# The opening of a two-block network: x in two column halves, and the bias vector moved behind the first weight unit

## What is computed

```
proj = x @ w_in                                   # 1024 x 2560
q_a, k_a, v_a, x_m, z_m = split(proj)
bias = rel_bias[rel_bucket(distance)]             # 32 buckets x 8 heads
logits = q_a . k_a * hd**-0.5 + bias
x_c = silu(causal_conv(x_m, conv_w, conv_b))
q_m, k_m = x_c per head @ w_qk_m;  v_m = x_m per head @ w_v_m
gates = concat(q_m, k_m, v_m) @ w_if + b_if
...
```

## Time and profile before

| What | Value |
|---|---|
| median of three runs | 2257.81 us (2256.44 to 2258.74) |
| profiled execution, its own time | 2260.36 us |
| span of its trace | 2257.3 us |
| mean granted clock of TensorE | 0.994 |
| VectorE, ScalarE and GpSimd busy | 77%, 59%, 12% of the span |
| bytes moved by DMA | 569.57 MB, mean 252 GB/s |

### The profile page before, as it was taken

How to read it: one execution, slowest core, us unless ns; L and a number is a source line. 1 busy time by engine, 2 the same in 40 slices (tenths; PEclk the granted TensorE clock), 3 DMA queues, 4 the chain that set the end, 5 groups by cost and what they waited for, 6 DMA issues and landing times.

```text
span 2257.3 us, 35008 instructions
## 1 busy us (share of the span) xinstructions
PE 2214.1 (98%) x13553; PEld 1946.6 (86%) x13553; DVE 1728.3 (77%) x1730; ACT 1333.3 (59%) x1226; POOL 265.5 (12%) x207
## 2 busy tenths in 40 slices
PE   8999999999999999999999999999999999999998
PEld 8999999999887888888888888787898999888997
DVE  5557544655788888888888888889788877798776
ACT  5643444464377777777777777676546444545444
POOL 2000000100000000000000000115193000590000
PEclk9999999999999999999999999999999999999999
DMA  9444655734599999999999999999633555434551
GB/s 295 143 141 160 205 186 185 235 127 147 174 330 360 377 368 364 377 362 378 366 376 364 374 365 377 350 362 375 221 127 113 197 175 187 152 115 160 183 195 47
DMA packets 309655, 569.57 MB, mean 252 GB/s; under 512 B 10322, under 2 KB 146244, under 8 KB 309488
## 3 DMA queue, kind: packets, MB, share of 16 engines
q1 hardware_dynamic: 303792, 548.53, 69.4%
q0 software_dynamic: 5776, 19.85, 2.7%
HBM read 562.56 MB, written 10.50 MB: 254 GB/s over the span
## 4 chain that ended last, share of the span: by engine, by line
PE 84%; POOL 5%; DVE 3%; ACT 3%; POOLq 2%; issue 1%; DMA 1%; DVEq 1%; ACTq 0%
PE ps L696 26%; PE ps L698 26%; PE ps L697 26%; POOL agT L678 3%; POOLq L677 2%; POOL tap L672 2%; DVE w_lo L1873 2%; ACT w_hi L1440 1%; PE ps L1137 1%; PE ps L763 1%; PE ps L747 1%; PE ps L910 0%; DMA xr<-rows,token_of 0%; PE ps L902 0%; PE ps L1120 0%
## 5 line engine op out<-in xcount | busy, mean ns | idle before, releaser
L1873 DVE TENSOR_TENSOR w_lo<-raw,w_hi 128x2048 fp32r<-128x2048 f32 x518 | 1194.9, 2313 | 311.7 <-ACT w_hi L1440 307.8
L1440 ACT ACTIVATE w_hi<-raw 128x2048 fp32r<-128x2048 f32 x518 | 985.8, 1908 | 330.8 <-PE ps L698 322.3
L696 PE MATMUL ps<-xT_hi,w_hi 128*128 128x256 f32 (+1 forms) x1712 | 488.6, 285 | 7.9 <-DVE xT_lo L1904 5.1
L697 PE MATMUL ps<-xT_lo,w_hi 128*128 128x256 f32 (+1 forms) x1712 | 484.0, 283 | 0.0
L698 PE MATMUL ps<-xT_hi,w_lo 128*128 128x256 f32 (+1 forms) x1712 | 484.0, 283 | 0.0
L696 PE MATMUL ps<-w_hi,xg_hi 128*128 128x512 f32 x896 | 360.5, 402 | 4.4 <-DVE w_lo L1873 4.4
L698 PE MATMUL ps<-w_hi,xg_lo 128*128 128x512 f32 x896 | 354.7, 396 | 0.0
L697 PE MATMUL ps<-w_lo,xg_hi 128*128 128x512 f32 x896 | 354.4, 396 | 0.0
L696 PEld LDWEIGHTS ps<-xT_hi,w_hi 128*128 128x128 f32 (+1 forms) x1712 | 326.3, 191 | 13.8 <-issue 7.4
L697 PEld LDWEIGHTS ps<-xT_lo,w_hi 128*128 128x128 f32 (+1 forms) x1712 | 326.4, 191 | 1.5
L698 PEld LDWEIGHTS ps<-xT_hi,w_lo 128*128 128x128 f32 (+1 forms) x1712 | 326.4, 191 | 0.4
(11 more groups left out here) (488 smaller groups left out, 2666.1 us busy)
## 6 DMA issues: line engine op xcount, KB each, us to landing
raw<-in_exp_w SPq DMA_DIRECT2D x336, 1024.0 KB, 6.1
raw<-in_ffn_w_up SPq DMA_DIRECT2D x44, 1024.0 KB, 5.1
raw<-in_w_in SPq DMA_DIRECT2D x41, 1024.0 KB, 5.9
raw<-in_ffn_w SPq DMA_DIRECT2D x33, 1024.0 KB, 5.1
raw<-in_ffn_w_down SPq DMA_DIRECT2D x22, 1024.0 KB, 5.4
raw<-in_w_gate SPq DMA_DIRECT2D x16, 1024.0 KB, 8.4
raw<-in_w_out SPq DMA_DIRECT2D x8, 1024.0 KB, 5.0
raw<-in_w_o SPq DMA_DIRECT2D x6, 1024.0 KB, 5.3
```

The source lines that it names most:

```text
L696: pe.matmul(out, lhs[0], rhs[0], start=first, stop=False)
L697: pe.matmul(out, lhs[0], rhs[1], start=False, stop=False)
L1440: act.activation(w_hi[:, u.const % SPL, 0:width], raw[:, u.const % RAW, 0:width], ACT.Copy)\
L1873: dve.tensor_tensor(w_lo[:, u.const % SPL, 0:width], raw[:, u.const % RAW, 0:width], w_hi[:, u.const % SPL, 0:width].bitcast(F32), ALU.sub ...
```

## The change

The two small tables leave the head of the sync queue and go behind the second weight half. x is loaded in two column halves of 512 KB, each ahead of one weight half, with a semaphore of its own for the second. `transpose_x` waits for the first half ahead of the first pair and for the second ahead of the third. The matmul for the bias vector moves from ahead of x to between `T(0)` and `T(1)`, into another PSUM bank (2 instead of 0), and TensorE no longer waits for its copy. ScalarE's copy moves behind the eviction of `T(0)`. GpSimd's program is untouched.

```diff
             sp.dma_start(cst[:], A["const0"]).then_inc(S_.ident_loaded, 16)
-            sp.dma_start(onehot_sb[:], A["onehot"]).then_inc(S_.table_loaded, 16)
-            sp.dma_start(relrow[:], A["rel_bias"]).then_inc(S_.table_loaded, 16)
-            sp.dma_start(x[:], A["x"][0].rearrange("(t p) d -> p t d", p=P)).then_inc(S_.x_loaded, 16)
+            x_half = lambda h: A["x"][0].rearrange("(t p) d -> p t d", p=P)[:, :, h * HALF:(h + 1) * HALF]
+            sp.dma_start(x[:, :, 0:HALF], x_half(0)).then_inc(S_.x_loaded, 16)
...
                               .then_inc(raw_landed[0] if half else S_.half_landed, 16)
+                            if half == 0:
+                                sp.dma_start(x[:, :, HALF:], x_half(1)).then_inc(S_.x_rest_loaded, 16)
+                        sp.dma_start(onehot_sb[:], A["onehot"]).then_inc(S_.table_loaded, 16)
+                        sp.dma_start(relrow[:], A["rel_bias"]).then_inc(S_.table_loaded, 16)
                         continue
...
                     if b % 2 == 0:
                         pe.wait_ge(S_.xn_ready, ready + (b // 2 + 1))
+                    if plain and b % 2 == 0:
+                        pe.wait_ge(S_.x_rest_loaded if b else S_.x_loaded, 16)
...
                 T(0, L * 12)
+                if L == 0:
+                    pe.wait_ge(S_.table_loaded, 32)
+                    pe.matmul(ps[0:HA, 2, 0:BUCKET_W], relrow[:], onehot_sb[:], start=True, stop=True).then_inc(S_.bvec_psum, 1)
                 T(1)
...
-            pe.wait_ge(S_.table_loaded, 32)
-            pe.matmul(ps[0:HA, 0, 0:BUCKET_W], relrow[:], onehot_sb[:], start=True, stop=True).then_inc(S_.bvec_psum, 1)
-            pe.wait_ge(S_.bvec_ready, 1)
-            pe.wait_ge(S_.x_loaded, 16)
...
                     out(n, xmT[:, 2 * n:2 * n + 2, CONV_K - 1:], bank(n, 2, S))
+                    if (L, n) == (0, 0):
+                        act.wait_ge(S_.bvec_psum, 1)
+                        act.activation(bvec[:], ps[0:HA, 2, 0:BUCKET_W], ACT.Copy).then_inc(S_.bvec_ready, 1)
...
-            act.wait_ge(S_.bvec_psum, 1)
-            act.activation(bvec[:], ps[0:HA, 0, 0:BUCKET_W], ACT.Copy).then_inc(S_.bvec_ready, 1)
```

## The result

| | median | ratio to before, 95% interval |
|---|---|---|
| before | 2257.81 us (7 runs) | |
| changed | 2268.63 us (7 runs) | 1.0045 [1.0034, 1.0055] |
| changed, run again (`after_again`) | 2269.70 us, before 2258.91 beside it | 1.0039 [1.0025, 1.0053] |

The change makes the kernel 10.8 us slower, in both measurements. The predicted time was 2266.4 us, in a range of 2259 to 2270. The trace read here is that of the repeat, since in the first traced execution of the changed kernel (2690.08 us, left out of the ratio) TensorE's mean granted clock was 0.752.

What follows compares the result with a forecast made beforehand. TensorE, busy 98% of the span, was taken as the bound, so the opening decides: `values` at 39.7 instead of 31.05, +8.6 us with the opening's 1.65 gain included, on the median 2257.8 gives 2266.4 us, range 2259 to 2270.

Steps and rivals of the forecast that it cites:

- part 1: Opening: x in halves lands and is transposed earlier, so T(0) ends at 17.4 instead of 19.07, a gain of 1.65 us.
- Part 2: Behind T(0): the bias vector's matmuls take 0.7 us on TensorE's path, costed at nothing because the wait for rows1 covers them.
- Part 3: GpSimd's queue before T(2): its chain starts 13.4 us later, TensorE idles about 7 us, `values` starts 8.6 us late.
- the two counts: Start of `values`: rows1 plus slow clock allow 38.8, the last b_if 39.7; the later decides, instead of 31.05.
- the second count: Before `values`: wqk, w_if and b_if are all there only when the last b_if lands, at 39.7 us.
- The rival of fast landings: GpSimd's small transfers at 19 to 31 us land in 2.0 us: 2257.7 us, no change; chance 0.15.
- The rival of useless halves: Opening: x's halves land together or late, no gain, everything 1.65 us later: +10.3 us, 2268.1; chance 0.11.
- The fixed 2.0 us: Opening loads: a fixed cost per transfer from the skill page, making x's second half an estimated 2 us late if paid in sequence.

Runs made afterwards that it cites:

- loads_ahead: Changed kernel, but GpSimd issues the ten loads (rows1, wqk, w_if, b_if) before waiting for the bias vector: 2258.24 us, ratio 0.9995 to the kernel before.
- vector_moved_alone: Kernel before with only the bias vector's matmul and copy moved behind T(0), x whole, tables at the head: 2270.85 us, ratio 1.0043.
- rows1_ahead: Changed kernel, but only the four loads of rows1 go ahead of GpSimd's wait for the vector: 2266.81 us, ratio 1.0031 to the kernel before.
- rows1_behind: Changed kernel, but wqk, w_if and b_if go ahead of GpSimd's wait and only rows1 stays behind: 2269.23 us, ratio 1.0050 to the kernel before.
- kept_busy: Changed kernel with 58 more matmuls, results unused, between T(1) and TensorE's wait for rows1: 2267.24 us, ratio 1.0040 to the kernel before.
- halves_alone: Kernel before with x in halves; tables stay at the queue's head, the vector's matmul ahead of x in PSUM bank 2, its copy not awaited: 2257.60 us, 0.9999.
- vector_between_busy: Changed kernel with ten loads ahead of GpSimd's wait, vector's matmul between x's transposes, tables before x's second half, ten extra identity matmuls: 2257.47 us, 0.9990.
- vector_between_few: Changed kernel with ten loads ahead of GpSimd's wait, vector's matmul between x's transposes, tables before x's second half, four extra identity matmuls: 2257.78 us, 0.9993.

## Why the prediction was right

**The mechanism** was the forecast one: GpSimd's queue waits for the late vector, and TensorE waits for what stands behind that wait. `loads_ahead` shows that the loss is gone when the loads stand ahead of that wait, `vector_moved_alone` that it is there without the halves. **The size** was 2.2 us short (8.6 forecast, 10.8 measured), so that the measured time lies near the top of the range: the gain of part 1 was taken too large, the time until rows1 landed and the slow clock too small, and the count that the forecast took for the later one was the earlier one.

**Part 1, the gain of the opening, was over-sized:** 1.65 us forecast, 0.53 measured. Two steps of it failed. x's second half landed at 8.9, not 8.1, so the second part of T(0) could start at 13.87 and not at 13.1: 0.77 us. The second weight half, too, landed at 10.5 and not 9.5; in the kernel before, with the tables ahead, it landed at 10.4. So the 0.9 us by which the queue started earlier were lost until then, and why is not shown. And I counted T(0)'s matmuls at 0.12 us, though I had used 0.24 for the transposes just before them: they ran on at 0.21 until 14.7, which cost 0.35 us more behind 13.87. Both vary from trace to trace: in the five traces read with this opening (`after_again`, `loads_ahead`, `rows1_ahead`, `rows1_behind`, `kept_busy`) x's second transposes start at 8.4 to 9.5 and T(0)'s last matmul at 17.97 to 18.73, a gain of 0.3 to 1.1 us, always below the forecast. The Trainium skill's page "TensorE: Matmul & The Clock Gate", section "What's actually happening", says that the throttled clock is the default and that activity releases it; the traces here agree (0.21 us before, 0.12 after, for the same matmul, while TensorE works), and the forecast had no term for it.

**Part 2, the vector's matmul on TensorE's path:** 0.7 forecast, 0.83 measured, and covered by the wait as said.

**Part 3, the chain.** The store was issued at 20.36 (19.1 forecast; T(0)'s last matmul was 1.1 later than the forecast 17.4, and the copy also had to wait for the vector's matmul) and took 6.0 us instead of 5.2; the rows took 5.0 (5.1 forecast); they landed at 33.2 instead of 31.2, and TensorE stood 7.8 us (7 forecast). The slow clock behind it cost 2.3 us where I had taken 1.6 from a shorter wait. The last b_if took 6.9 us and not 8.8. So of the two counts that I held against each other (38.8 for rows1 and the clock, 39.7 for b_if) the other one was later: rows1 and the clock at 41.6, b_if at 39.9. That b_if came as forecast is luck: it was issued 2.1 us later and took 1.9 us less. `kept_busy` and the two half moves show that the second count was real and close behind.

**The rival of fast landings** fell: at 20 to 33 us the store and the rows took 5.0 to 6.0 us and the last b_if 6.9, with the DMA engines at 1.08 to 1.11. The page "DMA: Bandwidth & Descriptors" of the Trainium skill also has, in its section "Latency and other measured facts", a memory latency of 0.2 us on average and 2 us under high load; the direction agrees with these runs, and the measured difference (2.0 us near 1620 us against 5 to 6) is larger. **The rival of useless halves** is partly true: the halves did land one by one (5.6 and 8.9), but the second landed late, and with the pace of T(0) two thirds of the gain were gone. (The fixed 2.0 us that the prediction held against the halves was fitted for GpSimd's transfers; the halves go through the sync queue, where the four pieces of x and the first weight unit landed 1.4 to 1.9 us apart.)

## What to carry to other kernels

When a producer is moved later, look at the queue of the engine that waits for it, not only at who needs its result: here the vector's own result was wanted some 20 us later, and ten loads that had nothing to do with it stood behind the wait. Put loads that depend on nothing ahead of the wait in a queue that issues in order, and price a small transfer by what it takes beside the traffic of its own stretch (here 5 to 6 us for what took 2.0 beside idle DMA engines). The stall of TensorE here was also paid for after it had ended, with 2.3 us on the lower clock; and a slow first stretch can eat what an earlier start gains, as in `halves_alone`.

## What the runs showed that I had not expected

- T(0) starts at the lower pace in the traces of all ten altered kernels, whatever had run before: with 16 transposes in a row (`vector_moved_alone`: 0.21 us apart until 16.6), with the vector's matmul at 3.3 us (`halves_alone`: until 15.7), with ten matmuls at the start (`vector_between_busy`: until 15.6), with four (`vector_between_few`: until 13.7). In the last two the second transposes had run at full pace (8 in 1.10 and 1.09 us) and T(0) behind them was slow again. The one trace of the kernel before had 0.12 from its first matmul on. What releases the clock here was not settled.
- The column of the granted clock says 1.00 for 5 to 10 and 10 to 15 us of the changed kernel, while its transposes took 0.24 us that take 0.14 at full pace in `vector_between_few` (8 in 1.94 and in 1.09 us), and T(0) ran at 0.21 us, the pace of T(2) at a granted clock of 0.50 (23 matmuls in 4.6 us): at the start of these traces the pace of equal instructions is the safer reading.
- A store of 12 KB took 6.0 us at 20 us where it had taken 5.2 at 5.7 us.
